# Lead-in of a two-mixer encoder layer: where x's second half lies, when z's products start, when the S5 parameters are loaded and turned

## The chip, the cores and the metric

One core of a Trainium2 chip runs one program. The metric is the device time of that program in microseconds (us), here the median of three executions. Five engines work side by side, each through its own list of instructions in order: TensorE (PE; its weight loads are shown as PEld), VectorE (DVE), ScalarE (ACT), GpSimd (POOL) and SyncE (SP), which issues DMAs. They wait for each other by semaphores. DMAs issued by SP and ScalarE go over the hardware queues q1 and q10, those of GpSimd over the software queue q0.

## The reference

x is 1024 tokens by 1024 columns in float32. One layer: h = RMSNorm(x) * norm_mix; proj = h @ W_in, whose columns are 512 for u (S5), 1536 for q, k and v, and 528 for z and the gates' raw values. The S5 mixer discretises a complex diagonal state per group, scans forward and backward, and applies GELU and a gate. The gated delta rule takes q, k, v through a convolution of five taps along the tokens and silu, scans in chunks, and is gated by silu(z). Then the output projection, a mixture of experts (32 experts, two per token) and a last norm:

```
h = rmsnorm(x, norm_mix);  proj = h @ w_in
lam_bar = exp(lam * exp(log_dt));  b_bar = (lam_bar - 1) / lam * b        # S5, per group and direction
y_A = glu(gelu(Re(c * scan(lam_bar, b_bar u)) + d u))
q, k, v = silu(conv(proj_qkv));  y_B = delta_rule(q, k, v, g, beta) * silu(z)
x = x + concat(y_A, y_B) @ w_out;  x = x + moe(rmsnorm(x))
```

The change touches the norm of x, the projection of z and u, and the S5 discretisation, all in the first tenth of the program.

## The kernel before

Tokens are cut into eight tiles of 128, x's columns into eight groups of 128. All products of the projection are done in three passes with split operands: every operand is kept as a high part (a rounded copy, made by ScalarE) and a low part (the rest, made by VectorE), and hi*hi, hi*lo and lo*hi are added (`three`, L335 to L337). The list of each engine is written out by hand in `in_projection`; its order is the order of the code in that engine's block.

SP issues four loads of x, two tiles each (L260), the norm's weights (L262), eight pieces of z's weights, one per column group (L264), the convolution's weights (L265), gate parameters (L863), and u's weights in four loads (L268). Behind them stand the stores of the S5 tables (`store_E`, L1834) and the convolution's weight loads.

GpSimd first makes the constants (the identity in its second step, L113, and 17 more steps up to L142), then issues the loads of the S5 parameters (`s5.loads`, L1484 to L1494: lambda, log dt, B in two loads, C in sixteen), then `t5.loads`.

ScalarE squares the eight tiles of x with a sum along the row (L499), and after each four tiles takes a square root (L502). VectorE turns the sums into scales (L680, L682) and multiplies the tiles (L685), four and four. TensorE then turns x: 16 groups n = 0 to 15 of four 128x128 transposes (L330), where groups 0 to 7 are the first four token tiles (one per column group) and 8 to 15 the last four. They go round four PSUM banks. ScalarE copies a group times the norm's weight as the high part (`hi_rows`, L456), VectorE makes the low part (`lo_rows`, L668). The weights of z are split in the same way (`hi_weights`, L476; `lo_weights`, L674). The tile `w_pieces`, in which most of them are written, lies in the same memory as `x_rows`: pieces 0 to 2 fit where the first four tiles of x were and are made after group 7 is turned, pieces 3 to 7 after group 15.

The z products go tile by tile, t = 0 to 7, into two PSUM buffers `proj_ps[0]` and `[1]`; ScalarE empties each by silu (`z_out`, L482 to L484). Tiles 0 to 3 need groups 0 to 7, tiles 4 to 7 need all. After z tile 0 TensorE turns the convolution's weights (L356) and S5's lambda and C (`s5.turn`, L1502, L1505) into the `turn_ps` banks. ScalarE and VectorE then work out S5: `act_part` 0 to 2 (L1512 to L1522: exponential, tanh, sines, each with its table load) beside `factors` (L1555 to L1644), part 3 copies C out (L1529). VectorE goes on with `t5.angles` and `t5.make_E` for four units u (L1892), which `turn_E` turns on TensorE (L1786) and SP stores; `t5.twiddle` makes sines on ScalarE (L1852 to L1856), which GpSimd stores (L1748). `make_G(0)` waits until the stores of all four twiddles are done. The u products follow z's, eight tiles of every eighth token; `g.sums` (L925 to L933) stands after u tile 5 and waits for `g.decays` on VectorE (L875 to L879), which stands after `make_G(0)`.

u's weights and later `uS` and the convolution's input lie in one tile, `conv_work`.

## Time and profile before

| | us |
|---|---|
| median of three executions (1408.2 to 1411.42) | 1410.66 |
| the profiled execution | 1412.43 |
| its span | 1410.7 |

| engine | busy us | share |
|---|---|---|
| TensorE | 1319.2 | 94% |
| VectorE | 1079.2 | 76% |
| ScalarE | 868.1 | 62% |
| GpSimd | 462.5 | 33% |

The profile is one execution on the chip. The span runs from its first instruction to its last; the rest of the execution's time lies around it. Each instruction carries a start and a duration, and where its engine stood idle before it, how long and which work ended the wait. A busy share is a mean over stages with different limits, so the stage of the change is read by itself.

### The profile page before, as it was taken

What the parts mean: (1) busy time and instruction counts of PE and PEld (TensorE: products, weight loads), DVE (VectorE), ACT (ScalarE), POOL (GpSimd) and SP (SyncE); (2) the same over time, 40 slices, a digit from 0 to 9 for tenths busy, and PEclk for the clock granted to TensorE, in tenths of its full rate; (3) what the DMA queues carried; (4) which work ended last, traced back from release to release, by engine and by line L of the source; (5) the groups of instructions that cost most, each with busy time, mean ns of one, the idle gap of its engine ahead of it and who ended that gap; (6) DMA issues with size and microseconds to landing.
All of it is one profiled execution on the core that took longest, in us unless ns stands there. A gap on an engine that the chain in (4) does not pass through costs nothing. (4 is left out here: it accounts for less than half of the span.)

```text
span 1410.7 us, 25141 instructions
## 1 busy us (share of the span) xinstructions
PE 1319.2 (94%) x8506; PEld 1113.9 (79%) x8506; DVE 1079.2 (76%) x1468; ACT 868.1 (62%) x1168; POOL 462.5 (33%) x508
## 2 busy tenths in 40 slices
PE   4999999987898889999998999999999999999995
PEld 3999778867888878758887788888888888888872
DVE  5795798684878748744666988888888888888856
ACT  7474345565566455463213877777777788777754
POOL 6020089108665637511200143333111111111125
PEclk9999999997999999999998999999999999999998
DMA  9175887512224119832103999999999999999956
GB/s 273 43 227 157 259 245 228 150 32 47 59 60 161 33 47 338 324 91 91 45 31 145 421 421 422 412 409 416 410 408 409 411 413 411 405 414 415 391 210 255
DMA packets 154825, 357.51 MB, mean 253 GB/s; under 512 B 43999, under 2 KB 100603, under 8 KB 127483
## 3 DMA queue, kind: packets, MB, share of 16 engines
q1 hardware_dynamic: 131899, 297.04, 55.9%
q0 software_dynamic: 14976, 40.43, 8.4%
q10 hardware_dynamic: 7872, 19.01, 3.4%
q8 instruction: 48, 0.79, 0.2%
q14 instruction: 30, 0.25, 0.1%
HBM read 287.64 MB, written 68.78 MB: 253 GB/s over the span
## 5 line engine op out<-in xcount | busy, mean ns | idle before, releaser
L2972 PE MATMUL gate_up_mm<-w_hi,gathered_T_hi 128*128 128x512 f32 x528 | 210.7, 399 | 1.1 <-DVE gathered_T_lo L3186 0.9
L2974 PE MATMUL gate_up_mm<-w_hi,gathered_T_lo 128*128 128x512 f32 x528 | 206.6, 391 | 0.0
L2973 PE MATMUL gate_up_mm<-w_lo,gathered_T_hi 128*128 128x512 f32 x528 | 206.4, 391 | 0.0
L3181 DVE TENSOR_TENSOR w_lo<-w_down,w_hi 128x2048 fp32r<-128x2048 f32 x66 | 148.5, 2290 | 54.0 <-ACT w_hi L3095 53.9
L3095 ACT ACTIVATE w_hi<-w_up 128x2048 fp32r<-128x2048 f32 x66 | 126.6, 1920 | 52.7 <-PE down_mm L3009 50.3
L3181 DVE TENSOR_TENSOR w_lo<-first_w_gate,w_hi 128x2048 fp32r<-128x2048 f32 x66 | 150.4, 2289 | 8.2 <-ACT w_hi L3095 8.2
L3181 DVE TENSOR_TENSOR w_lo<-w_up,w_hi 128x2048 fp32r<-128x2048 f32 x66 | 150.6, 2288 | 4.4 <-ACT w_hi L3095 0.6
L3095 ACT ACTIVATE w_hi<-first_w_gate 128x2048 fp32r<-128x2048 f32 x66 | 127.0, 1926 | 41.4 <-PE gate_up_mm L2974 27.4
L2847 POOL COPY gather_idx<-upto_pair 128x1 int32 x33 | 11.0, 335 | 425.6 <-PE x_turned L2962 425.6
L3095 ACT ACTIVATE w_hi<-w_down 128x2048 fp32r<-128x2048 f32 x66 | 123.9, 1916 | 38.7 <-issue 22.0
L2972 PEld LDWEIGHTS gate_up_mm<-w_hi,gathered_T_hi 128*128 128x128 f32 x528 | 99.6, 189 | 27.6 <-issue 8.3
L2974 PEld LDWEIGHTS gate_up_mm<-w_hi,gathered_T_lo 128*128 128x128 f32 x528 | 99.1, 188 | 21.4
L2973 PEld LDWEIGHTS gate_up_mm<-w_lo,gathered_T_hi 128*128 128x128 f32 x528 | 99.3, 188 | 18.9
L3007 PE MATMUL down_mm<-w_hi,hidden_T_hi 128*128 128x512 f32 x264 | 105.8, 401 | 0.2 <-DVE hidden_T_lo L3294 0.2
L3009 PE MATMUL down_mm<-w_hi,hidden_T_lo 128*128 128x512 f32 x264 | 103.1, 391 | 0.0
L3008 PE MATMUL down_mm<-w_lo,hidden_T_hi 128*128 128x512 f32 x264 | 103.0, 390 | 0.0
L2850 POOL DMA_INDIRECT gathered<-h_rows,gather_idx x33 | 75.0, 2271 | 26.3 <-POOL gather_idx L2847 26.3
L335 PE MATMUL proj_ps<-hT_hi,w_split 128*128 128x512 f32 x192 | 77.4, 403 | 0.0
L336 PE MATMUL proj_ps<-hT_lo,w_split 128*128 128x512 f32 x192 | 75.9, 395 | 0.0
L337 PE MATMUL proj_ps<-hT_hi,w_split 128*128 128x512 f32 x192 | 75.9, 395 | 0.0
L1766 POOL DMA_DIRECT2D s_rows_dram<-kv_rows x128 | 65.2, 518 | 10.4 <-DVE kv_rows L1983 10.4
L335 PE MATMUL proj_ps<-w_pieces,hT_hi 128*128 128x264 f32 (+1 forms) x176 | 59.2, 336 | 1.5 <-DVE w_pieces L674 1.5
(535 smaller groups left out, 3151.1 us busy)
## 6 DMA issues: line engine op xcount, KB each, us to landing
w_up<-in_expert_w_up SPq DMA_DIRECT2D x66, 1024.0 KB, 8.6
w_down<-in_expert_w_down SPq DMA_DIRECT2D x66, 1024.0 KB, 7.4
first_w_gate<-in_expert_w_gate SPq DMA_DIRECT2D x64, 1024.0 KB, 8.0
expert_rows_dram<-ones SPq DMA_DIRECT2D x32, 512.0 KB, 6.6
expert_rows_dram<-expert_out ACTq DMA_DIRECT2D x32, 512.0 KB, 8.3
x<-s_rows_dram SPq DMA_DIRECT2D x9, 1184.0 KB, 7.7
s_rows<-s_rows_dram SPq DMA_DIRECT2D x7, 1184.0 KB, 7.0
w_raw<-in_w_in SPq DMA_DIRECT2D x12, 512.0 KB, 5.3
```

The costliest lines, as they stand in the source:

```text
L335: pe.matmul(dst, left(0), right(0), start=k == 0, stop=False)
L336: pe.matmul(dst, left(0), right(1), start=False, stop=False)
L337: return pe.matmul(dst, left(1), right(0), start=False, stop=k == KT - 1)
L2850: pool.indirect_dma_start(out=xg[:, s, :], out_offset=None, in_=h_dram, in_offset=bass.IndirectOffsetOnAxis(ap=idx[:, s:s + 1], axis=0)).t ...
L2972: pe.matmul(dst, xT_hi[:, k, :], hi[:, at, cols], start=k == 0, stop=False)
L2973: pe.matmul(dst, xT_hi[:, k, :], lo[:, at, cols], start=False, stop=False)
L2974: mm = pe.matmul(dst, xT_lo[:, k, :], hi[:, at, cols], start=False, stop=k == KT - 1)
L3007: pe.matmul(dst, hT_hi[:, k, :], hi[:, at, cols], start=k == 0, stop=False)
L3008: pe.matmul(dst, hT_hi[:, k, :], lo[:, at, cols], start=False, stop=False)
L3009: mm = pe.matmul(dst, hT_lo[:, k, :], hi[:, at, cols], start=False, stop=k == KD - 1)
L3095: act.activation(hi[:, slot(s, j), :], flat(j), ACT.Copy).then_inc(S["piece_hi"], 1)
L3181: dve.tensor_tensor(lo[:, at, :], flat(j), hi[:, at, :].bitcast(F32), ALU.subtract).then_inc(S["piece_lo"], 1)
```

## The change

- x is loaded in five loads: tile 0, tile 1, then two tiles each. Tiles 4 to 7 go into the first half of `conv_work` instead of `x_rows`. All z weight pieces now wait for group 7 only, and u's weights, which share `conv_work`, are issued after group 15 is turned; they stand on SP's queue at the same place.
- The norm's weights are loaded by ScalarE's queue, as its first instruction, and a square root of one column stands ahead of the squares.
- GpSimd makes the identity, then issues the S5 loads, then makes the other constants.
- TensorE turns groups 0 to 10, then C, the convolution's weights and lambda, and then starts the z products. Groups 11 to 14 follow z tile 1, group 15 follows z tile 2. C is turned into `proj_ps[1]`, lambda into the fourth `turn_ps` bank beside the convolution's weights; z tile 1 waits until C is copied out.
- ScalarE: four weight pieces, C's copies (part 3), four pieces, rows 8 to 10, the convolution's weights, parts 0 to 2, z_out(0), z_out(1), rows 11 to 15.
- VectorE: all low weight pieces, rows 8 to 10, `factors`, rows 11 to 15, `powers` (the rest of what `factors` did), the angles. `angles(2)` stands behind the low parts of u's weights instead of ahead of them.
- The turn of E(1) goes from before u tile 0 to behind u tile 1, that of E(2) from behind u tile 2 to behind u tile 3. On ScalarE E_out(1) and the twiddles 2 and 3 move one u tile later.

```
--- before.py
+++ after.py
@@ -104,14 +104,18 @@
     return c
...
-def make_constants(pool, c, made):
-
-    step = Steps(pool, made)
+def make_identity(pool, c, step):
     step(pool.memset(c["ones"][:], 1.0))
...
                             pattern=[[1, P]], channel_multiplier=-1))
+def make_constants(pool, c, step):
+    one = c["ones"][:]
     step(pool.affine_select(out=c["upto"][0][:], in_=one, compare_op=ALU.is_ge, fill=0.0, base=0,
...
     step(pool.affine_select(out=c["upto"][1][:], in_=one, compare_op=ALU.is_ge, fill=0.0, base=0,
@@ -141,6 +145,9 @@
     step.done()
...
                             pattern=[[16, 8], [0, 16]], channel_multiplier=-1))
+X_LOADS = ((0, 1), (1, 2), (2, 4), (4, 6), (6, 8))
...
 def in_projection(nc, core, c, a, out, tb, y_dram, filled, s5_dram, g_dram, z_dram, a_dram, x_dram):
@@ -161,7 +168,16 @@
     raw = core.sb("w_raw", [P, 2 * KT * P])
...
     split = core.sb("w_split", [P, 2, 2, KT * P], F32R)
-    xs = out["x_rows"]
+    x_first, x_second = out["x_rows"][:, 0:4], work[:, 0:4 * D].rearrange("p (t n) -> p t n", t=4)
+    def x_tiles(first, end):
+        if first < 4:
+            return x_first[:, first:end]
+        return x_second[:, first - 4:end - 4]
+    def x_tile(t):
+        return x_tiles(t, t + 1)[:, 0]
     rows = [q_rows, kv[:, 0:TT], kv[:, TT:2 * TT]]
...
     split_flat = split[:].rearrange("p s w n -> p (s w n)")
@@ -172,6 +188,7 @@
     nrt = core.sb("qk_rt", [P, 2, H, TT])
...
     normw = core.sb("norm_mix_w", [P, KT])
+    first_root = core.sb("x_first_root", [P, 1])
     cw_rows = core.sb("conv_w_rows", [60, P])
...
     mm_ps = core.ps("proj_ps", [P, 2, 2, 512])
@@ -183,12 +200,13 @@
              "kk_out kk_st blk_ld k_rs along_ld f_diff f_exp n_sq n_rt n_inv inv_made base based x_st").split()
...
     made = S["made"]
-    x_ld = [core.sem(f"pj_x_ld{i}") for i in range(4)]
+    x_ld = [core.sem(f"pj_x_ld{i}") for i in range(len(X_LOADS))]
     z_ld = [core.sem(f"pj_z_ld{i}") for i in range(KT)]
...
     x_rows = a["x"].rearrange("b (t p) d -> p (b t) d", p=P)
+    loaded_with = {t: i for i, (first, end) in enumerate(X_LOADS) for t in range(first, end)}
     w_in = a["w_in"][0].rearrange("(k p) n -> p k n", p=P)
...
     ZC = 528
@@ -196,7 +214,7 @@
     CONV = 2 * KT
...
     s5 = s5_discretised(core, c, a, qT[:].rearrange("p h n -> p (h n)"), kT[:].rearrange("p h n -> p (h n)"), rho,
-                        bank[0:3])
+                        [bank[3][:, 64:512], mm_ps[:, 1, 0, :], mm_ps[:, 1, 1, :]])
     q_flat = q_rows[:].rearrange("p t n -> p (t n)")
...
                    [raw[:, 512 * n:512 * n + 512] for n in range(4)], sq[:], tr_ps, s5_dram)
@@ -256,14 +274,13 @@
                 sp.dma_start(raw_piece(CONV + j).rearrange("p (k n) -> p k n", k=KT),
...
-            for i in range(4):
-                sp.dma_start(xs[:, 2 * i:2 * i + 2], x_rows[:, 2 * i:2 * i + 2]).then_inc(x_ld[i], 16)
-            with nc.allow_non_contiguous_dma(reason="small parameters"):
-                sp.dma_start(normw[:], a["norm_mix"][0].rearrange("(k p) -> p k", p=P)).then_inc(S["par_ld"], 16)
+            for i, (first, end) in enumerate(X_LOADS):
+                sp.dma_start(x_tiles(first, end), x_rows[:, first:end]).then_inc(x_ld[i], 16)
             for k in range(KT):
...
             g.sync(sp)
+            sp.wait_ge(S["x_tr"], 2 * KT)
             for i in range(4):
...
             for u in range(4):
@@ -307,10 +324,12 @@
...
         def _(pool):
-            make_constants(pool, c, made)
+            constant_step = Steps(pool, made)
+            make_identity(pool, c, constant_step)
             with nc.allow_non_contiguous_dma(reason="small parameters"):
...
                 t5.loads(pool)
+            make_constants(pool, c, constant_step)
             t5.clear(pool)
...
             pool.wait_ge(S["summed"], 8)
@@ -321,15 +340,27 @@
         @block.tensor
...
             pe.wait_ge(made, 2)
-            for n in range(2 * KT):
+            def turn_x(n):
                 half, k = n // KT, n % KT
                 pe.wait_ge(S["x_h"], 4 * half + 4)
-                if n >= 4:
+                if n == 11:
+                    pe.wait_ge(S["cw_out"], 1)
+                    pe.wait_ge(s5.acts, 1)
+                elif n >= 4:
                     pe.wait_ge(S["h_lo"], n - 3)
...
                     mm = pe.transpose(bank[n % 4][:, t * P:(t + 1) * P],
-                                      xs[:, 4 * half + t, k * P:(k + 1) * P], c["ident"][:])
+                                      x_tile(4 * half + t)[:, k * P:(k + 1) * P], c["ident"][:])
                 mm.then_inc(S["x_tr"], 1)
+            for n in range(11):
+                turn_x(n)
+            s5.turn_C(pe)
+            pe.wait_ge(S["h_lo"], KT)
+            pe.wait_ge(S["cw_ld"], 16)
+            pe.transpose(bank[3][:, 0:60], cw_rows[:], c["ident"][0:60, 0:60]).then_inc(S["cw_turned"], 1)
+            s5.turn_lam(pe)
...
                 pe.matmul(dst, left(0), right(0), start=k == 0, stop=False)
@@ -339,6 +370,8 @@
             for t in range(TT):
...
                     pe.wait_ge(S["h_lo"], KT + 2 * t)
+                if t == 1:
+                    pe.wait_ge(s5.ev, 8)
                 if t >= 2:
...
                 for k in range(KT):
@@ -350,16 +383,13 @@
                     if t == TT - 1 and k < KT - 1:
...
                 mm.then_inc(S["projected"], 1)
-                if t == 0:
-                    pe.wait_ge(S["h_lo"], 2 * KT)
-                    pe.wait_ge(S["cw_ld"], 16)
-                    pe.transpose(bank[3][:, 0:60], cw_rows[:], c["ident"][0:60, 0:60]).then_inc(S["cw_turned"], 1)
-                    s5.turn(pe)
-                if t == 6:
-                    pe.wait_ge(S["cw_out"], 1)
-                    pe.wait_ge(s5.ev, 8)
+                if t == 1:
+                    for n in range(11, 2 * KT - 1):
+                        turn_x(n)
+                elif t == 2:
+                    turn_x(2 * KT - 1)
+                elif t == 6:
                     t5.turn_E(pe, 0)
-            t5.turn_E(pe, 1)
             for t in range(T5):
...
                 for k in range(KT):
@@ -368,8 +398,8 @@
                     mm = three(mm_ps[:, t % 2, 0, :], lambda w: hT[w][:, k, t:L:T5],
...
                 mm.then_inc(S["projected"], 1)
-                if t in (2, 4):
-                    t5.turn_E(pe, t // 2 + 1)
+                if t in (1, 3, 4):
+                    t5.turn_E(pe, (1, 3, 4).index(t) + 1)
                 if t == 5:
...
                     g.sums(pe)
@@ -449,16 +479,16 @@
...
         def _(act):
-            def hi_rows(half):
-                for n in range(KT * half, KT * half + KT):
-                    k = n % KT
+            def hi_rows(first, end):
+                for n in range(first, end):
+                    half, k = n // KT, n % KT
                     act.wait_ge(S["x_tr"], n + 1)
...
                 if n < KT:
-                    act.wait_ge(S["x_tr"], KT if n < 3 else 2 * KT)
+                    act.wait_ge(S["x_tr"], KT)
                 elif n < 2 * KT - 1:
...
                 elif n == 2 * KT - 1:
@@ -492,29 +522,35 @@
                                mm_ps[:, t % 2, 0, :].rearrange("p (g q) -> p g q", q=GC), ACT.Copy
...
+            with nc.allow_non_contiguous_dma(reason="small parameters"):
+                act.dma_start(normw[:], a["norm_mix"][0].rearrange("(k p) -> p k", p=P)).then_inc(S["par_ld"], 16)
+            act.wait_ge(made, 1)
+            act.activation(first_root[:], c["ones"][:, 0:1], ACT.Sqrt)
             for t in range(TT):
-                act.wait_ge(x_ld[t // 2], 16)
+                act.wait_ge(x_ld[loaded_with[t]], 16)
                 if t:
                     act.wait_ge(S["x_sq"], t)
-                act.activation(sq[:, 0:D], xs[:, t, :], ACT.Square, accum_out=ss[:, t:t + 1]).then_inc(S["x_sq"], 1)
+                act.activation(sq[:, 0:D], x_tile(t), ACT.Square, accum_out=ss[:, t:t + 1]).then_inc(S["x_sq"], 1)
                 if t % 4 == 3:
...
             act.wait_ge(S["par_ld"], 16)
-            hi_rows(0)
-            for n in range(3):
+            hi_rows(0, KT)
+            for n in range(4):
                 hi_weights(n)
-            hi_rows(1)
-            for n in range(3, KT):
+            s5.act_part(act, 3)
+            for n in range(4, KT):
                 hi_weights(n)
-            z_out(0)
+            hi_rows(KT, 11)
             act.wait_ge(S["cw_turned"], 1)
+            act.wait_ge(s5.m, 2)
             act.activation(cw[:].rearrange("p a n -> p (a n)"), bank[3][:, 0:60], ACT.Copy).then_inc(S["cw_out"], 1)
...
             s5.act_part(act, 2)
+            z_out(0)
             z_out(1)
-            s5.act_part(act, 3)
+            hi_rows(11, 2 * KT)
             for t in range(2, 5):
...
             t5.twiddle(act, 0)
@@ -524,16 +560,16 @@
             t5.E_out(act, 0)
...
                 hi_weights(n)
-            t5.E_out(act, 1)
             z_out(7)
             u_out(0)
+            u_out(1)
+            t5.E_out(act, 1)
             t5.twiddle(act, 2)
-            u_out(1)
+            u_out(2)
             t5.twiddle(act, 3)
-            u_out(2)
+            u_out(3)
             t5.E_out(act, 2)
             g.softplus(act)
-            u_out(3)
             u_out(4)
...
             u_out(5)
@@ -660,9 +696,9 @@
         def _(dve):
...
-            def lo_rows(half):
-                for n in range(KT * half, KT * half + KT):
-                    k = n % KT
+            def lo_rows(first, end):
+                for n in range(first, end):
+                    half, k = n // KT, n % KT
                     dve.wait_ge(S["h_hi"], n + 1)
...
                     dve.scalar_tensor_tensor(out=hT[1][:, k, dst], in0=bank[n % 4], scalar=normw[:, k:k + 1],
@@ -682,23 +718,23 @@
                 dve.reciprocal(ms[:, ts], rs[:, ts]).then_inc(S["x_ms"], 1)
...
                 for t in range(4 * half, 4 * half + 4):
-                    dve.tensor_scalar(xs[:, t, :], xs[:, t, :], ms[:, t:t + 1], None, ALU.mult).then_inc(S["x_h"], 1)
-            lo_rows(0)
-            for n in range(3):
+                    dve.tensor_scalar(x_tile(t), x_tile(t), ms[:, t:t + 1], None, ALU.mult).then_inc(S["x_h"], 1)
+            lo_rows(0, KT)
+            s5.first(dve)
+            for n in range(KT):
                 lo_weights(n)
-            lo_rows(1)
-            for n in range(3, KT):
-                lo_weights(n)
-            s5.first(dve)
+            lo_rows(KT, 11)
             s5.factors(dve)
+            lo_rows(11, 2 * KT)
+            s5.powers(dve)
             t5.begin(dve)
...
             t5.make_E(dve, 1)
-            t5.angles(dve, 2)
             for n in range(KT, CONV):
                 lo_weights(n)
+            t5.angles(dve, 2)
             t5.angles(dve, 3)
...
             g.begin(dve)
@@ -1493,22 +1529,26 @@
                         dst = self.Cn[:, 4 * i + 2 * d + half, NS * x:NS * x + NS]
...
-    def turn(self, pe):
+    def turn_C(self, pe):
+        pe.wait_ge(self.ld, 16 * self.N_LD)
+        for i in range(8):
+            mm = pe.transpose(self.banks[1 + i // 4][:, (i % 4) * P:(i % 4 + 1) * P], self.Cn[:, i, :],
+                              self.c["ident"][:])
+        mm.then_inc(self.m, 1)
+    def turn_lam(self, pe):
         DJ, ident = 2 * NP5, self.c["ident"]
-        pe.wait_ge(self.ld, 16 * self.N_LD)
         pe.wait_ge(self.v, 1)
...
         mm.then_inc(self.m, 1)
-        for i in range(8):
-            mm = pe.transpose(self.banks[1 + i // 4][:, (i % 4) * P:(i % 4 + 1) * P], self.Cn[:, i, :], ident[:])
-        mm.then_inc(self.m, 1)
...
         if part == 0:
-            act.wait_ge(self.m, 1)
+            act.wait_ge(self.m, 2)
             act.activation(lam.rearrange("p i n -> p (i n)"), self.banks[0][:, 0:3 * DJ], ACT.Copy
...
             act.wait_ge(self.acts, 1)
@@ -1522,7 +1562,7 @@
             act.activation(s[:, self.SH], s[:, self.TH], ACT.Sin, scale=0.5).then_inc(self.acts, 1)
...
             C = s5_cooked(self.cooked)["C"]
-            act.wait_ge(self.m, 2)
+            act.wait_ge(self.m, 1)
             for i in range(8):
...
                 dj = NP5 * d + 8 * half
@@ -1537,7 +1577,7 @@
                                   self.ldt.rearrange("p (a o) -> p a o", o=1).broadcast_to([2 * NP5, 2, NS])))
...
     def factors(self, dve):
-        DJ, s, lam, step, made = 2 * NP5, self.s, self.lam, self.step, self.made
+        s, lam, step, made = self.s, self.lam, self.step, self.made
         RE, DTC, AR, TH, TN, EM, EE, SN, SH, DR, DI, MM, T1, T2, QR, QI, TAU = range(17)
...
         TTo, STT = dve.tensor_tensor, dve.scalar_tensor_tensor
@@ -1610,6 +1650,16 @@
         ew(self.rho[:], s[:, EE], s[:, EE], ALU.mult)
...
         ew(self.rho[:], self.rho[:], self.rho[:], ALU.mult)
+    def powers(self, dve):
+        DJ, s, step, made = 2 * NP5, self.s, self.step, self.made
+        DR, DI, QR, QI = self.DR, self.DI, self.QR, self.QI
+        out = s5_cooked(self.cooked)
+        def ew(dst, x, y, op):
+            step.done()
+            step(dve.tensor_tensor(dst, x, y, op))
...
         step(dve.memset(out["pw"][:, 1, 0, :], 0.0))
```

## Rows read from the trace of the kernel before

**Rows 1.** Busy time by stretch: us, then busy us (instructions) of each engine
```profile
0.00:31.30 31.30, 11.49 (x63) 9.90 (x64) 17.06 (x28) 22.75 (x38) 21.78 (x47) 1.00 0.99 278
31.30:144.00 112.70, 111.23 (x700) 108.96 (x698) 87.51 (x146) 61.49 (x113) 12.40 (x14) 1.00 0.46 142
```

**Rows 2.** Timeline of ScalarE: start us, us, operation, out<-in, [idle before <-what ended it]
```profile
5.90 1.06 ACT L499 ACTIVATE square<-x_rows 128x1024 f32<-128x1024 f32 x1 [3.79 <-DMA x_rows<-in_x]
...
10.82 1.28 ACT L502 ACT_TABLE_LOAD   x1
12.11 0.20 ACT L502 ACTIVATE x_rs<-x_ms 128x4 f32<-128x4 f32 x1
...
19.48 2.42 ACT L456 ACTIVATE hT_hi<-turn_ps,norm_mix_w 128x512 fp32r<-128x512 f32 x4 [1.95 <-DMA norm_mix_w<-in_norm_mix]
...
46.58 1.47 ACT L1529 ACTIVATE kT<-turn_ps 128x128 f32<-128x128 f32 x8 [0.41 <-ACT ab L484]
...
57.08 0.39 ACT L482 ACTIVATE conv_silu<-proj_ps 128x264 f32<-128x264 f32 x1 [5.08 <-PE proj_ps L337]
...
62.90 0.39 ACT L482 ACTIVATE conv_silu<-proj_ps 128x264 f32<-128x264 f32 x1 [5.08 <-PE proj_ps L337]
...
100.63 1.14 ACT L1856 ACTIVATE qT<-qT,s_half_pi 128x1024 f32<-128x1024 f32 x1
```

**Rows 3.** Timeline of VectorE, same columns
```profile
10.83 0.48 DVE L680 TENSOR_SCALAR x_ms<-x_ss 128x4 f32<-128x4 f32 x1 [10.83 <-ACT square L499]
...
17.77 2.74 DVE L685 TENSOR_SCALAR x_rows<-x_rows,x_ms 128x1024 f32<-128x1024 f32 x4
20.43 5.95 DVE L668 SCALAR_TENSOR_TENSOR hT_lo<-turn_ps,norm_mix_w,hT_hi 128x512 fp32r<-128x512 f32 x8
26.29 1.94 DVE L674 TENSOR_TENSOR w_pieces<-q_rows,w_pieces 128x528 fp32r<-128x528 f32 x3
...
41.22 0.18 DVE L1555 TENSOR_SCALAR qT<-qT 128x32 f32<-128x32 f32 x1 [4.51 <-ACT qT L1515]
...
59.76 1.23 DVE L1892 TENSOR_TENSOR qT<-kT,s_ramp 128x1024 f32<-128x1024 f32 x1
...
66.02 1.22 DVE L1892 TENSOR_TENSOR q_rows<-kT 128x1024 f32<-128x1024 f32 x1
...
111.44 1.36 DVE L1892 TENSOR_TENSOR qT<-kT 128x1152 f32<-128x1152 f32 x1 [3.59 <-issue]
...
120.16 0.23 DVE L879 SCALAR_TENSOR_TENSOR tab_g<-gate_t,gate_par 128x64 f32<-128x64 f32 x1
```

**Rows 4.** Timeline of TensorE, same columns
```profile
81.92 1.91 PE L1786 MATMUL turn_ps<-ident,q_rows 128*128 128x128 f32 x16
...
84.96 0.61 PE L335 MATMUL proj_ps<-w_pieces,hT_hi 128*128 128x512 f32 x1 [1.13 <-DVE w_pieces L674]
...
124.20 0.53 PE L925 MATMUL turn_ps<-tab_g,upto_pair 128*128 128x32 f32 x4
```

**Rows 5.** DMA in 3:6, 14:16, 20:22 us; last row size, us to landing
```profile
DMA packets 312, 1.21 MB, mean 404 GB/s; under 512 B 16, under 2 KB 16, under 8 KB 312
...
q1 hardware_dynamic: 87, 0.16, 55.2%
q0 software_dynamic: 48, 0.16, 47.9%
...
q1 hardware_dynamic: 173, 0.32, 69.8%
...
qT<-in_s_b_re POOLq DMA_DIRECT2D x1, 256.0 KB, 9.6
```

**Rows 6.** Timeline of GpSimd, same columns as rows 2
```profile
1.36 0.29 POOL L115 TENSOR_SCALAR_AFFINE_SELECT upto_pair<-ones 128x128 f32<-128x128 f32 x1
...
6.13 0.74 POOL L1484 DMA_DIRECT2D qT<-in_s_lam_re  x1
...
7.89 1.74 POOL L1487 DMA_DIRECT2D qT<-in_s_b_re  x1
```

More of the change, by code:

```diff
@@ L114, in make_constants @@
                             pattern=[[1, P]], channel_multiplier=-1))
+def make_constants(pool, c, step):
+    one = c["ones"][:]
     step(pool.affine_select(out=c["upto"][0][:], in_=one, compare_op=ALU.is_ge, fill=0.0, base=0,
@@ L191, in in_projection @@
     x_rows = a["x"].rearrange("b (t p) d -> p (b t) d", p=P)
+    loaded_with = {t: i for i, (first, end) in enumerate(X_LOADS) for t in range(first, end)}
     w_in = a["w_in"][0].rearrange("(k p) n -> p k n", p=P)
@@ L451, in _, with hi_rows @@
         def _(act):
-            def hi_rows(half):
-                for n in range(KT * half, KT * half + KT):
-                    k = n % KT
+            def hi_rows(first, end):
+                for n in range(first, end):
+                    half, k = n // KT, n % KT
                     act.wait_ge(S["x_tr"], n + 1)
```

144 lines of the change are left out of this document (88 added, 56 removed).

## The prediction

> **What bounds the kernel now.** I read three views in this order. First the busy time by stretch [rows 1]: up to 31.3 us TensorE is busy for 11.49 us, then for 111.23 of 112.7 us. The lead-in is idle for TensorE and the projection is not, so a microsecond taken from the lead-in reaches the end if nothing inside the projection takes it back, and a microsecond added reaches the end whole. Next the timelines of ScalarE and VectorE over the lead-in [rows 2, 3]: ScalarE squares the tiles of x from 5.90 us, where the first megabyte lands, at 1.25 us a tile; VectorE scales the last four tiles from 17.77 us and begins the low parts of the turned x at 20.43 us. I call that moment T. TensorE turns x as fast as it is scaled. After T the work of VectorE sets the pace: 8 low parts in 5.95 us (0.74 each), weight pieces at 0.62 each (3 in 1.94) [rows 3]. Last the DMA queues [rows 5]: from 3 us the loads run at 404 GB/s, so the 4.2 MB of x (four loads of 1 MB) are through near 13.2 us. Only then do the S5 parameters of the software queue share the engines.
>
> **The time until T.** Four edits act on it.
> The first square starts when half a megabyte is there. At 404 GB/s that is 1.3 us before 5.90. It helps the first tiles alone, since all eight must be squared and the last two land together, before as after.
> The early square root takes one table load of 1.28 us out of the row of squares (10.82 to 12.11) [rows 2]. VectorE's small operation on the sums (0.48 us) must still pass before the root, so 0.8 us of it are saved. ScalarE went from the square before, through the load, to the next operation without a further gap. The Trainium skill (ScalarE: Activation LUTs, What ACT_TABLE_LOAD costs) adds a drain of about 1.38 us to such a load; by its figure 2.66 us would go, an estimate, but the trace shows no drain here and the row decides.
> The norm's weights leave the queue behind x. They held ScalarE until 19.48 us [rows 2], but VectorE was not free before 20.43, so this is worth nothing now; it would cost if x were early, and it will not be late on its own queue. Its small packets now run beside x instead of behind it: I take 0.6 us, between 0 and 1.
> The S5 parameters are loaded before the constants instead of behind them. Their first issue moves from 6.13 to about 1.4 us [rows 6], so all of them move by 4.7 us. The first load of B was issued at 7.89 us and landed 9.6 us later [rows 5, 6]; its packets show from 13 us on, and both halves of B take about 6 us. In the changed kernel that is from 8.3 to 14.3 us, inside x's loads. What the sharing costs: from 14 to 16 us the hardware queue moved 87 packets (0.16 MB) while the software queue moved 48 (0.16 MB) [rows 5]. An x packet is 3.9 KB (312 packets for 1.21 MB), so at the same 87 packets in 2 us x would run at 170 GB/s in place of 404. At 8.3 us x stands at 2.05 MB (5.6 us at 0.41, less the norm's share), at 14.3 us at 3.05 MB. The rest, 1.14 MB, runs beside the loads of C; the 173 packets in 2 us of 20 to 22 us [rows 5] would give 0.34 MB per us, and I take 0.30: 3.8 us. x is through at 18.1 us and landed at 18.6. Two squares follow (2.45), so the squares end at 21.05 us in place of 17.1, and T is 24.4 in place of 20.4: **4.0 us later**.
> Bounds: if the parameters take nothing from x, it lands at 13.7 to 14.3, the squares end near 16.3 and T is 19.6, 0.8 us earlier. If x gets only the hardware queue's bytes of that stretch (80 GB/s), it is through some 3 us later still, T near 27.5, plus 7. I take the packet count because the two queues went nearly packet by packet.
> The Trainium skill (DMA: Bandwidth & Descriptors, Queues, rings and completion order) says that each DMA engine goes round-robin between its queues a packet at a time; the 87 to 48 packets agree roughly, and the rule speaks against moving small-packet loads beside x.
>
> **From T to the end of the projection, counted from T.** The z products need only the first half of x, as x's second half no longer lies where the weight pieces are written. PE turns 11 of the 16 groups, C, the convolution's weights and lambda, and starts z tile 0 at T+7.0, when the first low piece is there (5.95 for the rows, 0.2 for the S5 copy, 0.7). Eight pieces at 0.62 are ready at T+11.1, so the tile is not held and ends at T+12.9. A z tile takes 5.82 us (57.08 to 62.90) [rows 2]. Before, tile 0 began at T+11. Then:
> - ScalarE: four pieces, C's eight copies (1.47) [rows 2], four pieces, three rows at 0.6, then lambda, a table load of 1.28 and the exponential: VectorE's factors start at T+13.9; before 41.22, which is T+20.8 [rows 3].
> - z tile 1 ends at T+18.7, four x groups at 0.45 (T+20.5), z tile 2 to T+26.4, the last group to T+26.8.
> - VectorE: factors to T+22.2, four low rows to T+25.1, then it **waits** 2.4 us for the last group, which ScalarE has copied at T+27.5. Behind this new wait stand powers, B, angles and E. It ends at T+28.3. From 41.22 to 59.76 the factors and powers took 18.5 us [rows 3]; the angles now start at T+38.5, before at T+39.3.
> - Two sets of angles (6.3, from 59.76 to 66.02) and E(0) (six operations of 1.23 with their gaps, 7.6) [rows 3] end at T+52.3. TensorE has ended z tile 6 at T+50.1 and waits 2.2 us for E(0), turns it (16 transposes, 1.8) [rows 4], and ends z tile 7 at T+60.
> - The third angles (3.1 us) stand behind u's weight pieces now. The first piece is ready at T+60.5; u tile 0 starts there, before at 84.96 [rows 4], T+64.5. That is 4.0 us earlier, of which 1.8 goes back, because the turn of E(1), which lay in that wait, now follows u tile 1.
> - u tiles at 5.88 us: TensorE would be ready for the gate sums at T+101.4, before at 124.20 [rows 4], T+103.8.
> - The last twiddles stand behind u_out(2) instead of u_out(1). They end at T+84.8; before 101.77 (100.63 and 1.14) [rows 2], T+81.3. G(0) on VectorE waits for their stores, and started 9.7 us after them at 111.44 [rows 3]. It now starts at T+94.5, the decays are ready 8.95 us later (120.39) at T+103.4, and TensorE **waits** 2 us for them. The gate sums start at T+103.5, 0.3 us earlier than before.
> u's weights are issued behind the last turn of x, near T+27 on SP. Nothing that is due stands behind them there (the E stores come at T+52), and they are needed at T+55: hidden, even at the 8 us that such loads take. The stores of the last E, behind which the convolution's weights are loaded, come 2 us earlier in T's count than before, so that load is not later than its user.
> Sum: plus 4.0, minus 0.3, **plus 3.7 us**; with the stores back sooner the wait at the gate sums goes and it is plus 1.7. The profiled execution took 1412.43 us (span 1410.7, the rest around it is untouched), so 1416.1 by its count. It lies 1.8 us above the median of 1410.66, to which I add the same: **1414.4**.
>
> **Rivals.** A: x keeps its pace beside the parameters. For it speaks that the first packets of B appear only when x is through, which might be the queue's order and not a delay of the issue; then B waits for x again. T is 19.6, and the end is minus 1.1 with G(0) as the bound, minus 3.1 with TensorE as the bound: 1407.6 to 1409.6. It decides against me if the last tile of x is landed before 14.7 us. B: x falls to the bytes seen, T plus 7: 1417.4. Against it: those packets were half the size. C: x is delayed by the share that the packets take and no more, about 2 us (B's 0.5 MB at the half share), and the stores land sooner: minus 0.3 to plus 1.7, so 1410.4 to 1412.4. D: the new wait for the last x group or the one for E(0) costs more than I count, because ScalarE is late with its silu copies: plus 2 more on my forecast, 1416.4.
>
> **Chances.** Forecast 0.42, its own range 1412.5 to 1416.0; A 0.25; B 0.08; C 0.15; D 0.10. A measurement of this kernel tells 0.2%, 2.8 us, from no change: 1407.9 and 1413.5. Below lie half of A and a few hundredths for gains that I don't see: 0.18. Within lie the other half of A, C, and a third of the forecast: 0.40. Above: 0.42. The range reaches from A to B: 1408.0 to 1417.0.
>
> **What would show it.** The time at which the last square starts, and the software queue's packets between 8 and 14 us: forecast about 19.8, A about 15. The first low row (T). VectorE idle before the last x group's low row. TensorE waiting before the turn of E(0) and before the gate sums. If T comes before 20.4 the forecast is wrong in its first step; if TensorE reaches the gate sums with no wait, in its last.

## The result, and the profile after

The changed kernel takes 1424.62 us (median of 8 runs, 1419.91 to 1425.79) against 1411.43 for the kernel before beside it (8 runs): ratio **1.0083, with a 95% interval of 1.0064 to 1.0101**, about 11.7 us slower. The profiled execution took 1420.19 us, its span is 1418.5, 7.8 more than before. The forecast was 1414.4, range 1408 to 1417: the sign was right, the forecast growth (3.7 us) less than a third of the measured one.

First the busy time by stretch, cut where the same work ends (T, the first low part of turned x, is 8.2 us later; the borders are 8.2 and 8.0 later than in rows 1):

```profile
0.00:39.50 39.50, 13.67 (x85) 12.92 (x86) 16.49 (x28) 21.81 (x45) 21.80 (x47) 1.00 0.69 190
39.50:152.00 112.50, 107.66 (x669) 105.35 (x668) 87.47 (x145) 58.95 (x104) 12.43 (x14) 1.00 0.49 152
```

The first stretch grew by 8.2 us and TensorE does hardly more in it (13.67 us busy; before 11.49 of 31.3 [rows 1]; z tile 0 has begun). The second, as long as before, has 3.6 us less TensorE work in it: what started early is spent on new waits. ScalarE (columns as in rows 2):

```profile
0.83 0.49 ACTq L526 DMA_DIRECT2D norm_mix_w<-in_norm_mix  x1
...
4.52 1.06 ACT L533 ACTIVATE square<-x_rows 128x1024 f32<-128x1024 f32 x1 [1.67 <-DMA x_rows<-in_x]
...
11.86 1.06 ACT L533 ACTIVATE square<-x_rows 128x1024 f32<-128x1024 f32 x1 [3.33 <-DMA x_rows<-in_x]
...
18.30 1.06 ACT L533 ACTIVATE square<-conv_work 128x1024 f32<-128x1024 f32 x1 [3.50 <-DMA conv_work<-in_x]
...
22.86 1.06 ACT L533 ACTIVATE square<-conv_work 128x1024 f32<-128x1024 f32 x1 [2.16 <-DMA conv_work<-in_x]
...
24.10 1.06 ACT L533 ACTIVATE square<-conv_work 128x1024 f32<-128x1024 f32 x1
...
112.98 1.13 ACT L1906 ACTIVATE qT<-qT,s_half_pi 128x1024 f32<-128x1024 f32 x1
```

Before, the first square began at 5.90 and the rest followed nearly without a gap; now each pair waits for its megabyte. The last one lands at 22.8 us, forecast 18.6. VectorE:

```profile
15.05 3.09 DVE L721 TENSOR_SCALAR x_rows<-x_rows,x_ms 128x1024 f32<-128x1024 f32 x4
25.28 0.17 DVE L716 TENSOR_SCALAR x_ms<-x_ss 128x4 f32<-128x4 f32 x1 [7.14 <-ACT square L533]
...
28.59 6.05 DVE L704 SCALAR_TENSOR_TENSOR hT_lo<-turn_ps,norm_mix_w,hT_hi 128x512 fp32r<-128x512 f32 x8
...
43.02 0.18 DVE L1595 TENSOR_SCALAR qT<-qT 128x32 f32<-128x32 f32 x1 [0.59 <-ACT qT L1555]
...
56.56 0.75 DVE L704 SCALAR_TENSOR_TENSOR hT_lo<-turn_ps,norm_mix_w,hT_hi 128x512 fp32r<-128x512 f32 x1 [2.62 <-ACT hT_hi L486]
...
67.54 1.23 DVE L1942 TENSOR_TENSOR qT<-kT,s_ramp 128x1024 f32<-128x1024 f32 x1
...
123.87 1.36 DVE L1942 TENSOR_TENSOR qT<-kT 128x1152 f32<-128x1152 f32 x1 [8.16 <-issue]
```

VectorE waits 7.14 us for the squares ahead of T = 28.59 (20.43 before [rows 3]), and 2.62 us for the last x group. TensorE's gate sums, then its waits from 20 to 145 us (line waited for: us in total, times, longest):

```profile
132.96 0.60 PE L961 MATMUL turn_ps<-tab_g,upto_pair 128*128 128x32 f32 x4 [2.10 <-DVE tab_g L915]
```

```profile
PE turn_ps L353 <- DVE hT_lo L704: 7.6, 1, 7.6
PE turn_ps L1836 <- DVE q_rows L1942: 2.3, 1, 2.3
PE turn_ps L961 <- DVE tab_g L915: 2.1, 1, 2.1
```

The gate sums start at 132.96, 8.8 us later than before [rows 4]. Why x is late stands in the DMA queues, here of 4 to 6, 10 to 12, 12 to 14 and 16 to 18 us (q1 carries x, q10 the norm's weights, q0 the S5 parameters; packets, MB, share of 16 engines):

```profile
q1 hardware_dynamic: 115, 0.44, 61.1%
q10 hardware_dynamic: 878, 0.00, 24.1%
...
q1 hardware_dynamic: 61, 0.22, 58.3%
q0 software_dynamic: 45, 0.12, 34.9%
...
q0 software_dynamic: 48, 0.20, 64.2%
q1 hardware_dynamic: 58, 0.24, 45.9%
...
q1 hardware_dynamic: 117, 0.42, 78.2%
q0 software_dynamic: 118, 0.13, 22.8%
```

Three slow stretches follow each other. From 4 to 6 us x moves 0.44 MB in place of the 0.81 that 404 GB/s [rows 5] give. From 10 to 14, beside B, it moves 0.46 MB in 4 us: 115 GB/s. From 16 to 18, beside C, 0.21 MB per us. (A share is the time of a queue's packets on the 16 engines; the shares of two queues can add up to more than 100%.) GpSimd issued B at 3.27 and C from 6.67 on:

```profile
3.27 1.74 POOL L1523 DMA_DIRECT2D qT<-in_s_b_re  x1
...
6.67 4.78 POOL L1530 DMA_DIRECT2D qT<-in_s_c_re  x8
```

### The profile page after: what moved, and what is told of

Same layout as the page of the kernel before. It is cut to its first block and busy times, and to the rows that moved or that the text cites. A ratio compares the mean times of both kernels' runs of the same rounds, so it can differ in the third digit from the quotient of the medians.

```text
span 1418.5 us, 25140 instructions
## 1 busy us (share of the span) xinstructions
PE 1314.8 (93%) x8506; PEld 1110.0 (78%) x8506; DVE 1079.4 (76%) x1468; ACT 865.0 (61%) x1167; POOL 464.8 (33%) x508
## 5 line engine op out<-in xcount | busy, mean ns | idle before, releaser
L3022 PEld LDWEIGHTS gate_up_mm<-w_hi,gathered_T_hi 128*128 128x128 f32 x528 | 99.6, 189 | 29.0 <-issue 8.2
```

Of the source, the lines that this page charges most:

```text
L3022: pe.matmul(dst, xT_hi[:, k, :], hi[:, at, cols], start=k == 0, stop=False)
```

## The experiments

The kernel before took 1406.4 to 1414.2 us on the four further chips (medians), so each kernel is given as a ratio to its runs on the same chip. The middle columns are read from each trace: the start of the last square, T, and the start of the gate sums, also counted from T. Spans of single traces are read with care: from the gate sums to the end they differ by up to 10 us (1278.1 to 1287.8) with no relation to the edits.

| kernel | last square | T | gate sums | from T | ratio (95%) |
|---|---|---|---|---|---|
| before | 15.93 | 20.43 | 124.20 | 103.8 | |
| changed | 24.10 | 28.59 | 132.96 | 104.4 | 1.0083 (1.0064–1.0101) |
| e4_changed_again | 24.65 | 29.14 | 133.55 | 104.4 | 1.0090 (1.0072–1.0107) |
| k3_changed_third | 24.11 | 28.60 | 134.48 | 105.9 | 1.0056 (1.0032–1.0080) |
| e1_s5_loads_late | 19.59 | 24.59 | 130.20 | 105.6 | 1.0058 (1.0038–1.0078) |
| e2_before_s5_early | 22.79 | 27.28 | 131.27 | 104.0 | 1.0049 (1.0030–1.0067) |
| e3_late_and_old_turns | 17.88 | 22.99 | 126.67 | 103.7 | 1.0002 (0.9985–1.0020) |
| f1_late_norm_behind_x | 15.18 | 19.67 | 129.24 | 109.6 | 1.0053 (1.0033–1.0072) |
| g1_all_three_mended | 15.81 | 21.94 | 121.50 | 99.6 | 0.9984 (0.9967–1.0000) |
| h1_before_norm_early | 17.51 | 22.41 | 126.18 | 103.8 | 1.0022 (1.0007–1.0036) |
| i1_changed_b_last | 20.36 | 25.03 | 130.75 | 105.7 | 1.0038 (1.0025–1.0050) |
| k1_b_last_norm_early | 17.11 | 24.11 | 123.95 | 99.8 | 0.9999 (0.9982–1.0017) |
| k2_b_last_norm_behind | 16.18 | 23.30 | 122.71 | 99.4 | 0.9997 (0.9979–1.0015) |
| l1_b_after_scaling | 16.12 | 20.61 | 120.16 | 99.6 | 0.9981 (0.9963–0.9999) |

**The S5 loads, in the changed kernel and alone in the kernel before.** My theory was that they delay x; the rival that the norm's weights beside x do.

```diff
 e1: changed kernel
             make_identity(pool, c, constant_step)
+            make_constants(pool, c, constant_step)
...
-            make_constants(pool, c, constant_step)
...
 e2: kernel before, with make_identity split off
-            make_constants(pool, c, made)
+            constant_step = Steps(pool, made)
+            make_identity(pool, c, constant_step)
...
                 t5.loads(pool)
+            make_constants(pool, c, constant_step)
```

> The changed kernel with one part undone: GpSimd makes all constants before it issues the S5 loads, as before the change. Theory 1 (the S5 parameters beside x delay x): B's packets again begin at 13 us, x is landed near 14.6 us (0.9 us later than before, for the norm's packets), the low rows start at T = 20.4 instead of 28.6, and the span falls by 6 to 8 us against the changed kernel, to 1410.5 to 1412.5. It will not reach the full 8.2, because C and the convolution's weights now land near 28 to 29 us, so z tile 0 starts near 29.5, up to 2 us later in T's count. Rival 2 (the norm's weights beside x, or the five loads, delay x): T stays above 26 and the span above 1416. Rival 3 (the new order after T is what costs): T falls but the span does not.

> The kernel before with this one part of the change alone: the identity, then the S5 loads, then the other constants. Theory 1: B's packets begin at 8.3 us, the last tile of x is squared near 23 us instead of 15.9, T is 27 to 28.5 instead of 20.4, and as the order after T is the old one, the whole of it is added: the span is 1417.5 to 1419. Rival 2: T stays near 20.4 and the span within 1 us of 1410.7.

Alone in the kernel before the early loads cost 6.9 us at T and 7.1 at the gate sums; the timed ratio, 1.0049, is 6.9 us. (The span of e2's own trace is 1410.0, not the 1417.5 to 1419 that I expected: it is 1278.7 us from its gate sums to its end, against 1286.5 in the trace of the kernel before. The ratio and the gate sums carry the reading.) They are the larger part of the loss. But undone in the changed kernel they give back only 4.0 of 8.2, where I expected all of it: x is still late in e1. From 4 to 6 us of that trace:

```profile
q1 hardware_dynamic: 142, 0.52, 64.2%
q10 hardware_dynamic: 904, 0.00, 25.1%
```

and the last megabyte of x is waited for until 18.34:

```profile
18.34 1.06 ACT L533 ACTIVATE square<-conv_work 128x1024 f32<-128x1024 f32 x1 [3.47 <-DMA conv_work<-in_x]
```

The norm's 1024 packets of 4 bytes cost x 0.29 MB, 0.7 us. That shifts the tail of x past 14 us, where B's packets now begin, and there each further packet is slow. The rival was half right: both loads matter.

**The norm's weights, alone and put back.**

```diff
 h1: kernel before; f1: e1 with the opposite move
-            with nc.allow_non_contiguous_dma(reason="small parameters"):      # SP, behind x
-                sp.dma_start(normw[:], ...).then_inc(S["par_ld"], 16)
...
+            with nc.allow_non_contiguous_dma(reason="small parameters"):      # ScalarE, first
+                act.dma_start(normw[:], ...).then_inc(S["par_ld"], 16)
```

> The kernel before with the norm's weights alone moved to ScalarE's queue, as its first instruction. Theory: its 1024 small packets take 0.3 to 0.4 MB of x's transfer from 2 to 6 us, so the end of x (near 13.2 us before) comes at 14.1 and falls among B's packets from 13 us on, and the last tiles land at 16 to 18.5 us. T is 22.5 to 24.5 instead of 20.43 and the time 2 to 4 us longer. Rival: 1024 packets cost their own 0.6 to 0.9 us and no more, T is 21.0 to 21.4.

> The changed kernel with both loads that ran beside x put back: the S5 loads behind the constants, and the norm's weights on SP's queue behind x. Theory (each of the two delays x, and together they make all of the late start): x is landed by 13.7 us, the last square starts near 15, the norm's weights land near 19.5, and the low rows start at T = 20.0 to 20.5, against 24.6 with the S5 loads late and the norm early, and 20.43 in the kernel before. Rival (x in the convolution's buffer, or the five loads, are slower to land): T stays above 22. By T's count the gate sums come at T+105.6, near 126, so the time is within 2.5 us of the kernel before's.

In h1 the norm alone costs 2.0 us at T and at the gate sums, and 1.0022 in time. Of the 2.0, 1.6 are x (the last square); 0.4 went on the scaling of its last four tiles, 3.14 us instead of 2.74, of which more below. In f1, with neither load beside x, T is 19.67: x in its new place, the early root and the first half megabyte are worth 0.8 us, as the lower bound of the forecast had it. That is the better of two traces: g1, below, has the same loads up to T, and its last square starts 0.1 us before that of the kernel before, not 0.8. But f1 is not faster than e1, against what I expected (T+105.6): its gate sums come at T+109.6. TensorE's waits in f1:

```profile
PE turn_ps L1836 <- DVE q_rows L1942: 2.3, 1, 2.3
PE turn_ps L961 <- DVE tab_g L915: 2.1, 1, 2.1
PE proj_ps L1536 <- DMA qT<-in_s_c_im: 1.7, 1, 1.7
PE turn_ps L364 <- DMA conv_w_rows<-in_gdn_conv_w: 0.8, 1, 0.8
```

With x early and the loads late, C is not there when the new order turns it, ahead of z tile 0, and VectorE behind it waits 1.14 and 4.15 us for x groups. The order that turns C early needs C early; loading C early delays x. The change contains both halves of that conflict.

**The order from T on.** e3 is e1 with the turns of E(1) and of the later E, the twiddles and E_out in the order of the kernel before. g1 is f1 with these turns, and the low part of the last x group moved to the middle of the S5 powers, so that VectorE works while ScalarE gets there.

```diff
 e3 and g1
+            t5.turn_E(pe, 1)
             for t in range(T5):
...
-                if t in (1, 3, 4):
-                    t5.turn_E(pe, (1, 3, 4).index(t) + 1)
+                if t in (2, 4):
+                    t5.turn_E(pe, t // 2 + 1)
...
 g1
-            lo_rows(11, 2 * KT)
-            s5.powers(dve)
+            lo_rows(11, 2 * KT - 1)
+            s5.powers(dve, lambda: lo_rows(2 * KT - 1, 2 * KT))
```

> As the first kernel (S5 loads behind the constants), and the turns of E, the twiddles 2 and 3 and their copies in the order of the kernel before. The wait of VectorE for the twiddles' stores (8.2 us in the changed kernel, 3.6 before) should go to 0 to 2 us, and TensorE's wait before the gate sums (2.1 us in the changed kernel) should go. If that wait is what takes the gain of the projection back, the span is 1.5 to 2.5 us below that of the first kernel, near 1409. If something behind the projection sets the time, it is the same as the first.

> As the last, with the turns of E and the twiddles in the old order, and the low part of the last x group moved from ahead of the S5 powers into their middle, so that VectorE has work while the group is turned. If VectorE's chain behind its wait (2.6 to 3.0 us in the runs so far) holds the projection, the first angles start near T+36.5 instead of T+39.2 to T+39.7, TensorE no longer waits for E(0), and the gate sums come at T+99 to T+101, near 120.5: 3 to 4 us faster than the kernel before. If T+103.7 stays, the wait was not what held it, and the time equals the kernel before's.

e3 reaches the gate sums at T+103.7 with no wait there, e1 at T+105.6: the moved twiddles cost 1.9 us. VectorE's wait for their stores is 3.6 us, as before the change, and not the 0 to 2 that I expected. (e3's T is 1.6 us earlier than e1's with the same lead-in: where x's tail lies among B's packets, T differs by that much from trace to trace, and a difference of 2 us between two single traces is weak.) g1 has no wait for E(0) either and is at T+99.6. Its time, 0.9984 (0.9967 to 1.0000), is 2.3 us below the kernel before, less than the 3 to 4 expected. So the early z products are worth some 4 us from T on, once neither VectorE's new wait nor the twiddles take them back. g1's T is 2.3 later than f1's, because the norm's weights landed at 21.2.

**B's packets against C's.** i1 is the changed kernel with B loaded behind C.

```diff
-        for i, n in enumerate(("s5_b_re", "s5_b_im")):
-            eng.dma_start(self.B[:, i], ...).then_inc(ld, 16)
         for i, n in enumerate(("s5_c_re", "s5_c_im")):
...
+        for i, n in enumerate(("s5_b_re", "s5_b_im")):
+            eng.dma_start(self.B[:, i], ...).then_inc(ld, 16)
```

> The changed kernel with B's two loads issued behind C's sixteen instead of ahead of them; all S5 loads still start at 1.5 us. Theory (B's packets of 64-byte pieces take most of the engines' time): C's loads run beside x from about 7 us on and cost it 1.5 to 3 us, B's packets come near 17 us when x is nearly through, and T is 23.5 to 26 instead of 28.6 to 29.1. Rival (any second queue beside x costs the same per microsecond): T stays at 28 or more.

T is 25.03, 3.6 us earlier than in the changed kernel. The queues from 12 to 14 us, now x beside C:

```profile
q1 hardware_dynamic: 136, 0.52, 89.0%
q0 software_dynamic: 103, 0.09, 17.1%
```

x moves 0.26 MB per us beside C here and 0.115 beside B in the changed kernel. In both, nearly packet goes by packet (136 to 103; 58 to 48). By the share (share x 2 us x 16 engines / packets) a packet of C takes 0.05 us of an engine and one of B 0.43, or 0.25 in the window from 10 us. B's packets are no smaller than x's: 0.20 MB in 48 are 4.2 KB, x's 0.24 in 58 are 4.1. They are gathered from pieces of 64 bytes, which may be why they are slow; no run changes the pieces, so that is not shown. Nor is the share the price. Beside C x lost 36% of its 0.81 MB in 2 us to a queue with a share of 17%, beside the norm's weights 46% to 24%, beside B 73% to 35% (from 10 us) and 70% to 64% (from 12 us).

The Trainium skill (DMA: Bandwidth & Descriptors, Queues, rings and completion order) has each DMA engine go round its queues a packet at a time. The trace agrees for x beside S5's queue, with 1.2 to 1.3 x packets for one of the other queue here and 117 to 118 from 16 to 18 us of the changed kernel. It does not for the norm's queue, as the profile counts packets: 878 to 115 of x. Why is open.

**Toward a better version.** k1 is g1 with B behind C on a semaphore of its own, waited for only in the powers, and the norm on ScalarE's queue. k2 is k1 with the norm behind x. l1 is k2 with B held until x is scaled.

```diff
 k1
+        for i, n in enumerate(("s5_b_re", "s5_b_im")):
+            eng.dma_start(self.B[:, i], ...).then_inc(self.b_ld, 16)
...
+        dve.wait_ge(self.b_ld, 32)
 l1
-                s5.loads(pool)
+                s5.loads(pool, lambda: pool.wait_ge(S["x_h"], 8))       # ahead of B's two loads
```

> The kernel with all three mended (S5 loads behind the constants, old order of the turns of E, the last x group's low part inside the S5 powers), with B loaded behind C on a semaphore of its own that only the powers wait for, and the norm's weights on ScalarE's queue. Theory (x's tail was stretched by B's packets, and C's landing near 28 us held the start of the z products): x's tail now meets C's packets, which take less; the last square starts near 16.5 to 17, T is 20 to 21.5; C is landed by 25, z tile 0 no longer waits for it; the gate sums come at T+99.5, near 120 to 121, 3.5 to 4 us before those of the kernel before. Rival (the convolution's weights, last in SP's queue near 29 us, hold z tile 0 in any case): the gate sums come at T+101 or later.

> As the first of this set, with the norm's weights on SP's queue behind x. x is landed by 13.7, and the norm's weights land at 16 to 18 us as B's packets no longer run beside them (19.5 to 21 with B there): T is 19.5 to 20.2, the earliest of all, and the gate sums near 119.5 to 121. If the norm's landing does not move, B's packets were not what delays it, and T is 20.5 to 22.

> The kernel with B loaded last and the norm's weights behind x, with one wait more: GpSimd issues B's two loads only when VectorE has scaled the eighth tile of x. In the kernel without this wait the four scalings of x's second half took 0.77 to 2.02 us each (5.30 together) while GpSimd issued B, 0.75 each (2.74) in kernels where it did not. Theory (issuing a load with many small pieces on GpSimd slows VectorE's scaling, which is why T was 23.3 and not 20.7): the four take 2.74 again, T is 20.5 to 21, and as B is needed only near 50 us, the gate sums come at 119.8 to 120.8, 3.4 to 4.4 us before those of the kernel before; ratio 0.996 to 0.999. Rival (something else slowed them, such as the transfers themselves): they still take over 4 us and T stays above 22.5.

k1 and k2 have the last square early (17.11, 16.18), but T, at 24.11 and 23.30, misses both forecasts: it is 7.0 and 7.1 us behind that square; in f1 it is 4.5. The 2.5 us went on VectorE, in k2 all of it in the scaling of x's second half; in k1 1.5 us there and 1.0 in the small operation on the sums ahead of it, 1.19 us instead of 0.17. All tiles of that line (min/median/max ns), first of k2, then of l1:

```profile
L722 DVE TENSOR_SCALAR x_rows<-x_rows,x_ms x4: 748/748/753, 11.5 to 13.5; 128x1024 f32<-128x1024 f32 x4
L722 DVE TENSOR_SCALAR conv_work<-conv_work,x_ms x4: 765/1374/2023, 18.1 to 22.6; 128x1024 f32<-128x1024 f32 x4
```

```profile
L722 DVE TENSOR_SCALAR conv_work<-conv_work,x_ms x4: 745/745/753, 18.0 to 19.9; 128x1024 f32<-128x1024 f32 x4
```

GpSimd issued B in k2 just then; in l1 it waits:

```profile
17.78 1.80 POOL L1532 DMA_DIRECT2D qT<-in_s_b_re  x1
19.52 1.89 POOL L1532 DMA_DIRECT2D qT<-in_s_b_im  x1
```

```profile
20.99 1.74 POOL L1533 DMA_DIRECT2D qT<-in_s_b_re  x1 [3.21 <-DVE conv_work L722]
```

The rival, that B's transfers slow the scaling, does not hold: in f1 B's packets move 0.18 MB beside it (16 to 18 us) and it takes 2.74 us; in k2 0.19 MB of the software queue move from 23 to 24 us, when the scaling is through. With the wait in l1 it takes 2.74 us again, T is 20.61, TensorE shows no wait from z tile 0 to the gate sums, which start at 120.16, 4.0 us before those of the kernel before. l1 takes 1402.85 against 1406.37 us, ratio **0.9981 (0.9963 to 0.9999)**: the one version here whose interval lies below 1, by little.

**The changed kernel again, twice.** In the first comparison the time grew by 11.7 us and the gate sums by 8.8, which might have been a stretch of low clock behind the projection. e4 could not decide it: its traced execution, with a mean clock of 0.981, was the shortest of its five (1413.31 us; median 1419.49).

Neither e4 nor k3 has an edit.

> The changed kernel unaltered. Its profiled execution took 1420.19 us, but six of eight executions took 1423.5 to 1425.8 with a mean TensorE clock of 0.971 to 0.975 instead of 0.977. Theory: the lead-in accounts for 7.8 us in all of them, and the 4.5 us more come from a stretch of lower granted clock behind the projection that most executions of the changed kernel have and few of the kernel before. If this profile falls in the longer group, the stretch of low clock is seen in it, most likely between 300 and 600 us; if every stretch is longer by a little, the theory falls.

> The changed kernel unaltered. The gate sums came 8.8 and 9.4 us later in its two traces, while its timed executions were 0.83% and 0.90% (11.7 and 12.7 us) slower. If the timed excess is real and lies in the lead-in, this trace may show T above 29 with the gate sums 10 to 12 us later; if it lies behind, the gate sums come near 133 and the ratio is again 1.007 to 1.010. If it was chance, the ratio is near 1.0065.

The three ratios make 11.7, 12.7 and 7.9 us (mean 10.8, each with some 3 us either way), the gate sums 8.8, 9.4 and 10.3 (mean 9.5). With these the two agree; that something behind the projection costs more as well is neither shown nor excluded. But k3 shows something else. Its trace from 81 to 85 us, and TensorE's turn of E(0):

```profile
81.00:85.00 4.00, 3.08 (x16) 3.08 (x17) 3.90 (x4) 1.90 (x5) 2.65 (x3) 0.65 0.97 278
```

```profile
81.92 3.46 PE L1836 MATMUL turn_ps<-ident,q_rows 128*128 128x128 f32 x16 [2.27 <-DVE q_rows L1942]
```

The same turn in the changed kernel's first trace:

```profile
81.37 1.97 PE L1836 MATMUL turn_ps<-ident,q_rows 128*128 128x128 f32 x16 [2.28 <-DVE q_rows L1942]
```

After the wait of 2.3 us for E(0) the granted clock is at 0.50 (1.2 GHz) from about 82.2 to 85.6 us in k3 and the 16 transposes take 3.46 us; in the first trace it is at 1.00 all through, and they take 1.97. Of seven traces with this wait five have the drop (e1, e3, f1, i1, k3: 2.61 to 3.63 us), two have not (the first and e4). Those of the changed order without it are at T+104.4 both, e1, i1 and k3 at T+105.6 to 105.9. So the new wait cost its 2.3 us, and 1.2 to 1.5 more where the clock fell.

## Why the prediction was wrong

By its own steps, on the first trace:

| step | forecast | measured |
|---|---|---|
| x's last megabyte landed | 18.6 | 22.8 |
| last square starts | 19.8 | 24.1 |
| T | 24.4 | 28.6 |
| z tile 0 starts | T+7.0 | T+7.3 |
| S5 factors start | T+13.9 | T+14.4 |
| wait for the last x group | 2.4, to T+27.5 | 2.6, to T+28.0 |
| angles start | T+38.5 | T+39.0 |
| TensorE waits for E(0) | 2.2, to T+52.3 | 2.3, to T+52.8 |
| last twiddles end | T+84.8 | T+85.5 |
| G(0) starts | T+94.5 | T+95.3 |
| gate sums, wait before them | T+103.5, 2.0 | T+104.4, 2.1 |

The mechanism was right and one term was mis-sized. **"x is through at 18.1 us and landed at 18.6 ... T is 24.4 in place of 20.4: 4.0 us later" is the step that failed**: T came 8.2 us later (8.7 and 8.2 in the other two traces). Of the 8.0 us between the forecast growth of 3.7 and the measured 11.7, this step is 4.2, the steps from T on are 0.9 (T+104.4 for T+103.5); 2.9 lie behind the gate sums or in the spread of the timing, and no run separates these.

Where the 4.2 came in shows in the queue's windows, added up. x had 1.82 MB at 8.3 us, forecast 2.05, and 2.68 at 14.3, forecast 3.05. These 0.37 MB are 1.2 us at the forecast pace of 0.30 MB per us. The last 1.51 MB then took some 7.1 us, 0.21 MB per us, instead of 5.0 at 0.30: 2.1 us, the largest part. The remaining 0.9 is the landing, which came some 1.4 us after x was through (near 21.4), not 0.5. The queues of the changed kernel from 8 to 10, 14 to 16 and 18 to 20 us:

```profile
q1 hardware_dynamic: 122, 0.46, 66.5%
q0 software_dynamic: 50, 0.18, 47.7%
...
q1 hardware_dynamic: 85, 0.34, 72.7%
q0 software_dynamic: 75, 0.09, 22.8%
...
q1 hardware_dynamic: 114, 0.47, 84.1%
q0 software_dynamic: 113, 0.11, 20.5%
```

The time of B's packets, forecast 8.3 to 14.3 us, was right. Three prices were too kind.
- Beside B I took 87 packets in 2 us at 3.9 KB, 170 GB/s. There were 122 in the first 2 us and then 58 to 61; from 8.3 to 14.3 us x moved 0.86 MB, 143 GB/s. The 87 packets of the old trace carried 1.8 KB each [rows 5] and took 0.20 us (55.2% of 32 engine-us over 87); x's own took 0.25 to 0.31 beside B, and 48 of B's took 64% of all engines, not 48%. A count of packets can't be carried over to packets of another size. Even so the bytes of that row, 80 GB/s, would have been too low: the stretch from 10 to 14 us had 115.
- Beside C I took 0.30 MB per us, from the 173 packets in 2 us of rows 5, by count again: they carried 1.8 KB each, x's 3.9. There were 85 to 117; from 14 to 20 us it was 0.17 to 0.24, and in i1, where C alone ran beside x, 0.22 to 0.26 from 8 to 18 us.
- For the norm I took 0.6 us, as its own cost; it was 0.37 MB, 0.9 us, and what it moves x's tail into costs more: 2.0 us alone in h1, and 3.3 to 4.9 in the changed kernel with the S5 loads late (e3 and e1 against f1).

Alone the two edits cost 6.9 and 2.0 us at T, and x's place and the root give 0.8 back: 8.1, and 8.2 is what they do together. That the sum fits so well is luck: the terms are single traces, 0.4 of h1's 2.0 is its slow scaling, and the norm costs 2.0 in one kernel and 3.3 to 4.9 in another. The early root did save 0.7 us in f1, where the fifth square starts 1.91 us behind the fourth and 2.57 before the change; the forecast had 0.8. With the megabytes late it hides behind the wait for x.

From T on each step is off by less than 1 us, and about half of that is there from the weight pieces on (VectorE idle 0.65 us between the fourth and the fifth). The clock after the wait for E(0) was not in the forecast at all; it added nothing in the first trace and some 1.5 us in the third.

Of the rivals, A (x keeps its pace) is refuted by e2 alone. B (T plus 7) had nearly the right size for the wrong reason: x beside B never fell to 80 GB/s, and by the forecast's own numbers 80 in place of 170 GB/s for 6 us is 0.54 MB, 1.8 us at 0.30 MB per us and not 3, so B's price should have been T plus 5.8. C is refuted with A. D, that the new waits cost more than counted, holds in part, though not by its reason (ScalarE late with its copies): in k3 it is the clock, and f1 shows that with x early it would have been 5 us, as C is not there. The chance of slower was 0.42 and should have been higher: both unknown paces rested on packet counts of smaller packets, the one beside B at the upper of its two bounds, and nothing in the old trace spoke for that.

## What to carry to other kernels

Where a stage waits for a bulk load, moving another load beside it is not free even if the bytes are few. Neither its bytes nor its share of the engines gives the price; take it from a window in which the bulk load itself runs beside it, and ask into what the tail of the bulk load is pushed. An edit of order (C turned early) can need the very load that delays it; measure both halves. A new wait of TensorE costs more than its length if the granted clock falls after it, as in five of seven traces here.

## What the runs showed of the hardware

- GpSimd's issue of B slows VectorE's tensor_scalar beside it: 765 to 2023 ns a tile against 745 to 753, 5.30 us against 2.74 for four in k2, 4.22 in k1 and 3.88 in i1 (x's first half). The issues of C, from 7.9 to 17.8 us in k2, ran beside the first half's tiles at 748 ns. Beside the end of C's issues and that of s_d it is less than B's but not nothing: 3.09 us in the changed kernel (767 to 872 ns a tile), 3.14 to 3.34 in e1, e3 and h1, with one tile of 1085 to 1089 ns each. The Trainium skill (SBUF — State Buffer, Who interferes with whom) has VectorE and GpSimd share a pair of ports that one holds for its whole instruction while the other is blocked, tensor_scalar among those that can ask for it. k2 against l1 agrees with it for B; why most of C's did no harm is open.
- 1024 packets of 4 bytes on another hardware queue, 25% of the engines by their own share, took x from 0.81 MB in 2 us to 0.44 to 0.52 in the changed kernel and e1.
- After the same wait of 2.3 us the granted clock fell to 0.50 (1.2 GHz) in five of seven traces and stayed at 1.00 (2.4 GHz) in two.
